# First branch as seven block products, its weights' operands made during the projection

## What is computed

```python
h = _rmsnorm(x, norm_g) * (1 + scale[:, None]) + shift[:, None]
z = h @ w_in                      # q, k, v, gates, low-rank decays, u, gate_b, mg_a, mg_b
...                               # gated linear attention in two directions -> o
o = _rmsnorm(o, gla_norm_g).reshape(B, T, GLA_VDIM) * jax.nn.silu(gate_a)
y_a = o @ w_proj_a                # the first branch: 2304 x 1024 by 1024 x 1024
...                               # Fourier mixing -> four
y_b = four @ w_proj_b             # the second branch
merged = jax.nn.sigmoid(mg_a) * y_a + jax.nn.sigmoid(mg_b) * y_b
x = x + gate[:, None] * (merged @ w_out)
```

## Time and profile before

| | us |
|---|---|
| median of 3 runs | 1938.8 (1936.61 to 1941.88) |
| profiled execution | 1940.98 |
| its span, first to last instruction | 1939.2 |
| TensorE busy | 1888.0 (97%) |
| VectorE, ScalarE, GpSimd busy | 1131.0, 908.8, 626.9 |
| mean granted TensorE clock | 0.993 |

### The profile page before, as it was taken

The page is one execution under the profiler, slowest core; times in us unless marked ns, Lnnn a source line. Parts: engine busy times, 40 slices in busy tenths (PEclk is TensorE's granted clock), DMA queues, the critical chain, the costliest instruction groups (busy, mean ns, idle before and its releaser), DMA issues.

```text
span 1939.2 us, 29861 instructions
## 1 busy us (share of the span) xinstructions
PE 1888.0 (97%) x10345; PEld 1741.0 (90%) x10345; DVE 1131.0 (58%) x2043; ACT 908.8 (47%) x1925; POOL 626.9 (32%) x660
## 2 busy tenths in 40 slices
PE   7899999999999999999999998999999999999997
PEld 2899999999999999999999996888887888888885
DVE  4978887784444435644444445666666422448787
ACT  3565667653445455444456225777743110024343
POOL 0136634044334513344333000000931023433644
PEclk9999999999999999999999999999999999999999
DMA  7578778967788889778788959556447665745443
GB/s 286 209 272 293 283 283 316 372 249 253 252 282 278 257 313 342 240 234 271 264 267 293 360 191 362 206 225 237 161 171 248 212 229 187 279 157 177 163 163 130
DMA packets 166256, 483.24 MB, mean 249 GB/s; under 512 B 14624, under 2 KB 51930, under 8 KB 156636
## 3 DMA queue, kind: packets, MB, share of 16 engines
q1 hardware_dynamic: 152284, 430.99, 64.0%
q10 hardware_dynamic: 13824, 50.34, 6.5%
HBM read 316.64 MB, written 155.20 MB: 243 GB/s over the span
## 4 chain that ended last, share of the span: by engine, by line
PE 66%; DVE 5%; DMA 3%; POOL 3%; issue 2%; ACT 1%; SPq 0%; DVEq 0%; ACTq 0%; POOLq 0%
PE bank L2406 33%; PE bank L2741 10%; PE bank L2706 5%; PE bank L2767 4%; PE bank L2570 3%; PE bank L2537 3%; PE bank L2635 2%; PE bank L2548 1%; PE bank L2559 1%; DMA x_st<-in_x 1%; POOL h_lo L1069 1%; DMA qd<-qk_dec 1%; DVE me_op L2079 1%; PE bank L2620 1%; PE bank L2578 1%
## 5 line engine op out<-in xcount | busy, mean ns | idle before, releaser
L2406 PE MATMUL bank<-h_hi,w_op 128*128 128x384 f32 x4032 | 1051.6, 336 | 15.0 <-DVE h_lo L1752 5.0
L2406 PEld LDWEIGHTS bank<-h_hi,w_op 128*128 128x128 f32 x4032 | 731.9, 188 | 20.8 <-issue 19.8
L2406 PE MATMUL bank<-h_lo,w_op 128*128 128x384 f32 x2016 | 674.9, 335 | 0.0
L2406 PEld LDWEIGHTS bank<-h_lo,w_op 128*128 128x128 f32 x2016 | 379.7, 188 | 0.0
L1746 DVE TENSOR_TENSOR w_op<-w_raw,w_op 128x512 fp32r<-128x512 f32 x240 | 187.4, 781 | 95.5 <-ACT w_op L1245 92.2
L1094 POOL TENSOR_TENSOR decs<-decs,qk_s 128x192 f32<-128x192 f32 x192 | 123.3, 678 | 334.6 <-ACT decs L1319 334.3
L1245 ACT ACTIVATE w_op<-w_raw 128x512 fp32r<-128x512 f32 x240 | 149.2, 623 | 159.3 <-PE bank L2406 156.4
L2767 PE MATMUL bank<-ow_op,me_op 128*128 128x512 f32 x756 | 173.0, 390 | 3.5 <-DVE u4o L2323 3.3
L2741 PE MATMUL bank<-in_a,pwa 128*128 128x512 f32 x768 | 174.3, 389 | 0.0
L2767 PEld LDWEIGHTS bank<-ow_op,me_op 128*128 128x128 f32 x756 | 141.4, 188 | 34.8 <-issue 5.8
L2741 PEld LDWEIGHTS bank<-in_a,pwa 128*128 128x128 f32 x768 | 144.1, 188 | 29.9
(11 more groups left out here) (265 smaller groups left out, 2761.7 us busy)
## 6 DMA issues: line engine op xcount, KB each, us to landing
w_op<-wt_dram SPq DMA_DIRECT2D x192, 512.0 KB, 5.6
wt_dram<-w_op ACTq DMA_DIRECT2D x96, 512.0 KB, 4.6
w_raw<-in_w_in SPq DMA_DIRECT2D x48, 768.0 KB, 6.2
w_raw<-in_w_in SPq DMA_DIRECT2D x24, 1024.0 KB, 6.7
qk_dec<-decs SPq DMA_DIRECT2D x48, 384.0 KB, 6.4
mg_dram<-outs SPq DMA_DIRECT2D x24, 768.0 KB, 7.5
swap<-qk_s SPq DMA_DIRECT2D x48, 192.0 KB, 5.7
v_dram<-outs SPq DMA_DIRECT2D x24, 384.0 KB, 4.7
```

What stands on the lines that cost most here:

```text
L2406: ins = pe.matmul(bnk, w_op[slot][:, part, k, :], h[:, j, k, :], start=(first and k == 0 and part == 0 and h is h_hi), stop=(k == HK - 1 a ...
```

## The change

The first branch becomes a block product too: 3 passes (`NA`) of 768 tokens, each 7 steps, a step being one product for 4 output parts (`product_of`): 12 matmuls of 384 columns per part, on 8 banks, four for each of two groups of accumulations. A pass has 16 merged tiles of 384 tokens. VectorE makes the four token sums (`sum_tokens`), the low parts (`low_op`), the quarter sums and gate products (`merge`); ScalarE the high parts (`high_op`) and copies of three products (`copy_a`); GpSimd adds the second branch's tile in place.

The operands of `w_proj_a` and of `w_out` are made in 56 jobs in the second and third pass of the projection, one every 5 products. A job makes a quarter of an operand, 128 x 512: ScalarE's queue loads one to four terms of 256 KB (`load_job`, `load_job_last`), VectorE sums them (`sum_job`), ScalarE rounds (`high_job`), VectorE makes the low part (`low_job`), ScalarE's queue stores both, 512 KB, to `jw_dram` (`store_job`). Two job buffers alternate. They lie in what the weights' sums used in the first pass.

SyncE then loads whole operands of 2.1 MB (`load_weights`): five for the first branch during the second, two behind it, and the seven of `w_out` during the last pass of the first branch, each into a place whose product is done. The splits and sums of `pwa`, `in_a` and `ow` and their loads are gone. Buffers of the last stages get other places; `u4o` now lies over gate slots 4 and 5, so the second quarter sum of the first out block waits for the stores of these slots.

```diff
+PASS = 768
+HP = PASS // 2
+NA = TOK // PASS
+ORDER_A = (0, 4, 1, 2, 5, 3, 6)
+TILE_OF = {1: (0, 0), 4: (0, 1), 5: (1, 1), 6: (1, 0)}
+NMERGE = 4 * len(TILE_OF) * NA
+TERMS_OF = {0: (0,), 4: (1,), 5: (2,), 2: (3, 0), 3: (3, 2), 1: (2, 3, 0), 6: (1, 2, 3, 0)}
+JOBS = [(matrix, part, j) for matrix in range(2) for part in range(4) for j in range(7)]
+JOB_STEP = 5
...
+        w_slot = [place(at, f"w_slot{n}", [P, 4, 2, 512], F32R) for n, at in enumerate(A_WEIGHTS)]
+        op_a = [[place(at + 6144 * q, f"op_a{n}{q}", [P, HK, HP], F32R) for q in range(2)] for n, at in enumerate(A_OPS)]
+        top = place(171008, "top", [P, KT, HP])
+        bottom = place(183296, "bottom", [P, KT, HP])
+        tok1 = place(195584, "tok1", [P, HK, HP])
+        tok2 = place(201728, "tok2", [P, HK, HP])
...
+        def job_at(p, w, j, lag):
+            t, behind = divmod(NPROD * (NW * (p - 1) + w) + j - lag, JOB_STEP)
+            return t if p and behind == 0 and 0 <= t < len(JOBS) else None
...
+            def load_weights(matrix, i):
+                k = i % 4
+                if matrix or i >= 4:
+                    sp.wait_ge(s_wr[k], 16 * (SLOT_LOADS[k] + (i // 4 if not matrix else (7 - k + 3) // 4 + i // 4)))
+                j = ORDER_A[i] if not matrix else i
+                sp.dma_start(w_slot[i][:, :, :, :].bitcast(F32), jw_dram[matrix, j].rearrange("c p q n -> p c q n")).then_inc(s_wr[k], 16)
...
+                if m in (2, 4, 8, 16):
+                    load_weights(0, (2, 4, 8, 16).index(m) + 1)
+                if m == 29:
+                    sp.wait_ge(s_bil, GROUPS * NB)
+                    load_tokens_a(0, 0)
+                    load_tokens_a(0, 1)
...
+            load_weights(0, 5)
+            load_weights(0, 6)
+            for s in range(GATE_SLOTS):
+                sp.wait_ge(s_mest[s], 16 * GATES_B[s])
+            for k in range(GATE_SLOTS):
+                load_merge(k)
+            def load_out_weights(i):
+                sp.wait_ge(s_y, product_a(NPROD * (NA - 1) + i, 3))
+                load_weights(1, i)
+            for k in range(NMERGE):
+                p, at = divmod(k, 16)
+                s = k % GATE_SLOTS
+                if p == NA - 1:
+                    if at == 0:
+                        load_out_weights(0)
+                    elif at == 4:
+                        load_out_weights(2)
+                        load_out_weights(3)
+                sp.wait_ge(s_me, k + 1)
+                j, t = merge_place(k)
+                sp.dma_start(me_dram[j, :, t], mg_a[s][:, :]).then_inc(s_mest[s], 16)
+                if k >= 2 and k + 4 < NMERGE:
+                    b = k - 2
+                    sp.wait_ge(s_mest[b % GATE_SLOTS], 16 * (GATES_B[b % GATE_SLOTS] + b // GATE_SLOTS + 1))
+                    load_merge(k + 4)
+                if p < NA - 1:
+                    if at == 3:
+                        sp.wait_ge(s_s, summed_a(p, 4))
+                        load_tokens_a(p + 1, 0)
+                    elif at == 8:
+                        sp.wait_ge(s_hl, OPS_LOW + NPROD * p + NPROD)
+                        load_tokens_a(p + 1, 1)
+                else:
+                    if at in (2, 6, 10, 14):
+                        load_out_weights({2: 1, 6: 4, 10: 5, 14: 6}[at])
+                    elif at == 3:
+                        sp.wait_ge(s_s, summed_a(p, 4))
+                        load_me(0)
+                    elif at == 12:
+                        sp.wait_ge(s_ml, me_made(0, 6))
+                        load_me(1)
...
-                pool.tensor_tensor(me_st[s][:, 0:n], mg_a[s][:, 0, 0:n], mg_a[s][:, 1, 0:n], ALU.add).then_inc(s_me, 1)
+            for k in range(NMERGE):
+                s = k % GATE_SLOTS
+                pool.wait_ge(s_yg, NTILE + k + 1)
+                pool.tensor_tensor(mg_a[s][:, :], mg_a[s][:, :], mb_a[s][:, :], ALU.add).then_inc(s_me, 1)
...
+            def load_job(t):
+                matrix, part, j = JOBS[t]
+                slot, terms = t % 2, job_terms(t)
+                if t == 0:
+                    act.wait_ge(s_wlo, split_count(NW - 1, NPROD - 1))
+                if t >= 2:
+                    act.wait_ge(s_jst[slot], 16 * (t // 2))
+                w = io[("w_proj_a", "w_out")[matrix]]
+                for q, term in enumerate(terms[0:2]):
+                    act.dma_start(job[slot][:, 1 - q, :].bitcast(F32), w[term][:, part]).then_inc(s_wr[slot], 16)
+                if len(terms) > 2:
...
+                    act.dma_start(job_x[:, :], w[terms[2]][:, part]).then_inc(s_wr[2], 16)
+            def load_job_last(t):
+                matrix, part, j = JOBS[t]
+                if len(job_terms(t)) == 4:
+                    act.wait_ge(s_jl, job_steps(t) + 1)
+                    act.wait_ge(s_wr[t % 2], 16 * (slot_loads(t) - 1))
+                    act.dma_start(job[t % 2][:, 0, :].bitcast(F32), io[("w_proj_a", "w_out")[matrix]][job_terms(t)[3]][:, part]
+                                  ).then_inc(s_wr[t % 2], 16)
+            def high_job(t):
+                act.wait_ge(s_wr[t % 2], 16 * slot_loads(t))
+                act.wait_ge(s_jl, job_steps(t + 1) - 1)
+                act.activation(job[t % 2][:, 0, :], job[t % 2][:, 1, :].bitcast(F32), ACT.Copy).then_inc(s_jh, 1)
+            def store_job(t):
+                matrix, part, j = JOBS[t]
+                act.wait_ge(s_jl, job_steps(t + 1))
+                act.dma_start(jw_dram[matrix, j, part], job[t % 2][:, :, :].bitcast(F32)).then_inc(s_jst[t % 2], 16)
+            def job_act(p, w, j):
+                for lag, do in ((8, store_job), (6, high_job), (4, load_job_last), (0, load_job)):
+                    t = job_at(p, w, j, lag)
+                    if t is not None:
+                        do(t)
...
+            def high_op(step):
+                p, i = divmod(step, NPROD)
+                if step >= 2:
+                    act.wait_ge(s_y, product_a(step - 2, 3))
+                else:
+                    act.wait_ge(s_y, (NTILE - 8, NTILE)[step])
+                if i in (2, 3, 4, 5):
+                    act.wait_ge(s_s, summed_a(p, {2: 2, 3: 1, 4: 4, 5: 3}[i]))
+                else:
+                    act.wait_ge(s_og[i == 6], 16 * (p + 1))
+                act.activation(op_a[step % 2][0][:, :, :], op_raw(i), ACT.Copy).then_inc(s_hh, 1)
+            def copy_a(step, c):
+                p, i = divmod(step, NPROD)
+                to = (u4a if i == 3 else u2a)[c]
+                act.wait_ge(s_y, product_a(step, c))
...
+                act.activation(to[:, :], a_bank(c), ACT.Copy).then_inc(s_p1, 1)
...
+            def sum_job(t, q):
+                out, terms = job[t % 2][:, 1, :].bitcast(F32), job_terms(t)
+                if q >= len(terms):
+                    return
+                other = job_x[:, :] if q == 2 else job[t % 2][:, 0, :].bitcast(F32)
+                dve.wait_ge(s_wr[t % 2], 16 * (slot_loads(t) - (len(terms) == 4 and q < 3)))
+                if q == 2:
+                    dve.wait_ge(s_wr[2], 16 * third_loads(t))
+                if q > 1:
+                    dve.wait_ge(s_jl, job_steps(t) + q - 1)
+                dve.tensor_tensor(out, out, other, ALU.add if q == 2 else ALU.subtract).then_inc(s_jl, 1)
+            def low_job(t):
+                dve.wait_ge(s_jh, t + 1)
+                x = job[t % 2][:, 1, :]
+                dve.tensor_tensor(x, x.bitcast(F32), job[t % 2][:, 0, :].bitcast(F32), ALU.subtract).then_inc(s_jl, 1)
+            def job_dve(p, w, j):
+                for lag in (7, 6, 3):
+                    t = job_at(p, w, j, lag)
+                    if t is None:
+                        continue
+                    if lag == 7:
+                        low_job(t)
+                    elif lag == 6:
+                        sum_job(t, 3)
+                    else:
+                        sum_job(t, 1)
+                        sum_job(t, 2)
...
+            def sum_tokens(p, n):
+                a11, a12, a21, a22 = top[:, 0:HK, :], top[:, HK:KT, :], bottom[:, 0:HK, :], bottom[:, HK:KT, :]
+                sa, sb = tok1[:, :, :], tok2[:, :, :]
+                out, x, y, op = ((sa, a21, a22, ALU.add), (sb, sa, a11, ALU.subtract), (a21, a21, a11, ALU.subtract),
+                                 (sb, a12, sb, ALU.subtract))[n]
+                if n == 0:
+                    dve.wait_ge(s_og[1], 16 * (p + 1))
+                    dve.wait_ge(s_og[0], 16 * (p + 1))
...
+            def merge(step, c):
+                p, i = divmod(step, NPROD)
+                if i not in TILE_OF:
+                    return
+                k = merged(p, i, c)
+                s = k % GATE_SLOTS
+                dve.wait_ge(s_y, product_a(step, c))
+                if i == 4:
+                    src = a_bank(c)
+                else:
+                    src = (u4a if i == 5 else u2a)[c][:, :]
+                    dve.wait_ge(s_p1, copied_a(p, {1: 0, 5: 3, 6: 2}[i], c))
```

(52 more changed lines are left out.)

349 lines of the change are left out of this document (136 added, 213 removed).

## The result

The changed kernel takes **1994.3 us** (median of four runs, 1991.99 to 1996.73) against 1939.1 of the kernel before beside it: a ratio of 1.028 [1.027, 1.030], 55 us slower, where 1931.5 us had been predicted and 1951 was the end of the range. The profiled execution took 1995.0 us, its span is 1993.0 (before 1939.2).

A forecast was written before the change was run, and what follows sets the result against it. TensorE, busy 97% of the span, was taken to bound the kernel. The terms -22.3 + 2.5 + 4 + 1.5 + 7 = -7.3 us, taken off the median of 1938.8, gave 1931.5 us, range 1917 to 1951.

The forecast's parts named there:

- The products: First branch: 1008 matmuls of 384 columns take 174.9 us against 197.1, -22.3 us.
- The start: Start of first branch: first low part stands on VectorE behind the second branch's multiplies, so TensorE starts later, +2.5 us.
- (a) The backlog at the end of the second pass: Projection, end of second pass: job bytes exceed the DMA rate, delaying output stores, +4 us (0 to 14).
- (b) Waits in ScalarE's and VectorE's queues: Projection: waits for job transfers delay work TensorE needs, showing only at the third pass's start, +1.5 us (0 to 4).
- the sign of it: Projection: prediction called itself wrong if ScalarE's waits for job stores reach TensorE in ordinary windows; no size given.
- queues cost more: Projection rival: 32 jobs or 21 steps each start a product 0.2 to 0.3 us late, +6, 1937.5 us; chance 0.18.
- The way into the out stage: First out block: 17.0 MB in SyncE's queue delay the last merged store and the u4o add, +7 us (0 to 12).
- DMA bounds the passes: Projection rival: DMA below 374 GB/s bounds the second pass; +19, 1958 us; chance 0.20.

The follow-up runs named there:

- e7: Changed kernel without its 56 jobs (last stages load stored operands instead), with the ways into the two last stages mended: 1934.9 us, ratio 0.997.
- e2: Changed kernel with the jobs' loads and stores only, no sums, roundings or low parts, a constant buffer stored: 1945.7 us, ratio 1.003.
- e1: Changed kernel without its 56 jobs; operands of the same number and size loaded from the projection's stored operands: 1940.6 us, ratio 1.000.
- e3: Changed kernel with the jobs' roundings, sums and low parts only, on zeros, without job transfers: 1944.3 us, ratio 1.003.
- e5: Changed kernel without the 56 job stores; loads, sums, roundings and low parts stay: 1945.4 us, ratio 1.004.
- e6: Changed kernel without the 112 job loads; stores and ScalarE's wait for each stay, operations run on zeros: 1948.4 us, ratio 1.005.
- e9: e7 without the seven 2 MB loads of the out weights' operands: 1919.1 us, ratio 0.989.
- e10: Changed kernel, nothing left out, with one job every six products instead of five, positions within a job unchanged: 1968.9 us, ratio 1.016.
- e12: Changed kernel with longer lags within jobs, last stages mended as in e7, and jobs kept out of the second pass's end: 1962.7 us, ratio 1.011.

## Why the prediction was wrong

**The products**, -22.3: right in kind. 1008 matmuls in one stage, 174.9 forecast, 179.9 measured; 1.8 of the rest are the two waits above, and most of what is left is the clock behind the wait at the start (below). With the first of these waits gone and the second at 1.0 us (e7, 1559.1 to 1736.9) it is 177.8.

**The start**, +2.5: measured 5.0. The low part did stand behind the multiplies, but those were late: the gate tiles waited behind the three operands and the tokens. I had priced that at 0 (bound 3) because TensorE has eight banks; VectorE, which had to get through all tiles before the low part, has none. VectorE's timeline:

```profile
1604.50 0.42 DVE L2368 TENSOR_TENSOR mg_b<-bank,mg_b 128x256 f32<-128x256 f32 x1 [5.53 <-DMA mg_b<-mg_dram]
...
1610.28 3.42 DVE L2241 TENSOR_TENSOR op_a<-top,op_a 128x1536 fp32r<-128x1536 f32 x2
```

**(a) The backlog at the end of the second pass**, +4 (0 to 14): the bytes alone cost 5 us, there and nowhere else (e2). For the bytes, place, mechanism and size were right. The changed kernel loses 20.6 us at that place, so most of its loss there is not the backlog by itself.

**(b) Waits in ScalarE's and VectorE's queues**, +1.5 with bounds 0 to 4: **the step that failed.** The changed kernel is 50.4 us late at the end of the projection; e1 is late by 4.0 too, the bytes add 5.3 (e2), the operations 1.4 (e3): some 40 are left for it. Three errors in it. The store's landing was taken from a row of a pass with less traffic (4.6 us; with the jobs it is 7.0). The slack of 4 to 6 us was granted to each wait separately, though the waits stand in one chain, from store to load to sum to rounding to low part, across two engines that run in program order; e5 and e6 show that each alone does fit, with half of the bytes, and together they don't. And the bound was an argument about one visit, where 56 visits follow each other 11 us apart: what counts is whether an engine's work and its waits fit in each period, and in 20 of 55 they don't (6 + 8 against 11 in the one shown). The text did name the sign of it (ScalarE's waits for job stores reaching TensorE in ordinary windows), and the rival "queues cost more" was priced at +6 for want of that sum.

**The way into the out stage**, +7 (0 to 12): measured 13.5, mechanism right. The queue's bytes do set it (e9); the last merged store releases u4o:

```profile
1808.60 0.56 DVE L2342 TENSOR_TENSOR mg_a<-u2a,mg_a 128x384 f32<-128x384 f32 x1 [7.88 <-DMA mb_a<-meb_dram]
1818.46 0.69 DVE L2419 TENSOR_TENSOR u4o<-bank,u2o 128x512 f32<-128x512 f32 x1 [8.71 <-DMA me_dram<-mg_a]
```

17.0 MB were divided by 392 GB/s. From the start of step 18 (1764.7) to the landing of the last merged tile (1818.3) the DMA engines moved 19.0 MB at 353 GB/s: 53.6 us instead of 44.7. The rate takes some 5 us of that (17.0 MB at 353 are 48.2 us instead of 43.4), the 2 MB that weren't counted most of the rest. TensorE came to product 5 after 41.2 us instead of 38.6, so 6.5 us of it show.

**The rivals.** "DMA bounds the passes", priced at +19 and 1958, was the only one on the right side. Its 407 us for the second pass at 340 GB/s even look like the 399.6 measured, but its mechanism isn't this one: e2 moves the same bytes in 377 us, and e10 runs TensorE without a gap at a share of 0.97 between 500 and 700 us. No case came near 1994.

**What stays open.** Why every version with all steps of a job there loses 8.8 to 20.6 us between windows 39 and 48, even where ordinary windows lose next to nothing: e1 loses 2.4 there, the bytes 5.7 more, the operations nothing, and e12 shows that the cost moves with the jobs. The traces show one thing that sets this stretch apart: the two engines have long waits of their own there. In the kernel before, ScalarE stands 16.1 us for the loads of the next pass's tokens (`x_st`), and VectorE 22.5 us for the squares that ScalarE makes of them; in e10 these are 19.5 and 20.2 us, and VectorE's 25 us of job waits come on top. That fits the sum of work and waits, but no run tests it, and which of the waits carries the loss wasn't separated. No version that makes all its operands beats the kernel before; e7's 1934.9 without jobs leaves 4 us for all 56 of them.

## What to carry to other kernels

A background job that passes from a load over two engines to a store and back needs a sum of its own: for each period, and not on average, each engine's work plus *all* its waits for the others, with landing times under the added traffic. Test it by giving each job one more step of room; if the time falls at the same bytes, it was the waits. A wait that is harmless alone says nothing about two of them. And when TensorE's work is shortened in a stage that also takes in its successor's weights, ask first whether those bytes still fit in the shorter stage.

## What the runs showed of the hardware

The granted clock falls after short waits, and that comes on top of what the wait costs. Stretches of the changed kernel, after the 5.0 us before 1612.1, after the 13.5 before 1819.3, and around one of 1.9 us at 603:

```profile
1612.10:1622.00 9.90, 9.88 (x41) 9.90 (x42) 6.69 (x4) 1.48 (x3) 0.00 (x0) 0.70 0.97 374
...
1819.30:1829.00 9.70, 9.70 (x36) 7.86 (x37) 9.63 (x15) 4.14 (x7) 0.41 (x1) 0.82 0.46 183
...
600.00:610.00 10.00, 8.08 (x40) 7.75 (x39) 6.31 (x15) 5.11 (x12) 0.64 (x2) 0.83 0.70 224
```

Each mixes the engine's two levels, 1.2 and 2.4 GHz; the stretches behind them are at 1.00 again. In the first, 41 matmuls ran where the 10 us from 1622 on, at 1.00, hold 59: about 3 us more, behind a wait of 5. In the projection the clock's 11.8 us come on top of 31.7 us of added waits, a third of their price again.

A VectorE subtraction of 128x512 elements gets longer while GpSimd works: in the kernel before, 0.69 us at 783.76 with GpSimd idle, 2.09 us at 793.62 with GpSimd making a sum for the next pass. The changed kernel has such subtractions of 2.10 us at 825.74 and 2.33 at 835.15, and VectorE is busy 13.9 of 16.9 us from 818.3 on. This is work and not waiting, but it can explain little of the loss at the pass's end: of the 20.6 us, 3.8 are lost from window 45 on, where it lies.
